# Gathered rows in other homes, weights that wait for a later gather, and a moved wait on the matrix engine

## What is computed

```python
def peer_ffn(x, wq, keys, u, v):
    qry = (xt @ wq).astype(f32).reshape(t, PEER_HEADS, 2, PEER_DK // 2)
    sub = jnp.einsum('thpd,pnd->thpn', qry, keys.astype(f32))
    s_top, i_top = lax.top_k(sub, PEER_TOPK)
    ...
    score, pos = lax.top_k(cand_s, PEER_TOPK)
    idx = jnp.take_along_axis(cand_i, pos, axis=-1)
    gate = jax.nn.softmax(score, axis=-1)
    ...
        act = jax.nn.gelu(jnp.einsum('td,thkd->thk', xb, u[ib]).astype(f32), approximate=False) * gb
        return jnp.einsum('thk,thkd->td', act, v[ib].astype(f32))
    ...
# the third block's input norm and projection, whose weights follow the last gather
h = rms_norm_2(x, g_mix[l])
qa, ka, va, qd, kd, vd, qm = jnp.split(h @ w_in[l], IN_SPLITS, axis=-1)
```

## Time and profile before

| | before |
|---|---|
| median of 3 runs (lowest, highest) | 2308.37 us (2306.19, 2309.63) |
| the profiled execution | 2306.09 us |
| its span, first to last instruction | 2304.3 us |
| busy: PE, DVE, ACT, POOL | 78%, 56%, 37%, 29% of the span |
| moved by the DMA engines | 920.49 MB, mean 399 GB/s |
| of it the gathers' queue (q0) | 549.70 MB |
| TensorE clock granted, mean | 0.853 |

### The profile page before, as it was taken

One profiled execution on the slowest core, in us unless ns is written; L12 is line 12 of the kernel. 1 busy time (PEld: TensorE's weight loads), 2 busy tenths in 40 slices (PEclk: granted clock), 3 DMA queues, 4 the chain that ended last, 5 costly groups with the idle time before them and its releaser, 6 DMA issues.

```text
span 2304.3 us, 30881 instructions
## 1 busy us (share of the span) xinstructions
PE 1789.9 (78%) x11196; PEld 848.4 (37%) x11196; DVE 1298.3 (56%) x3217; ACT 850.6 (37%) x2292; POOL 659.1 (29%) x606
## 2 busy tenths in 40 slices
PE   9999877695797777588779666877779997766666
PEld 4655521161352343153336112343327553222222
DVE  4878887668757766866776867555442331111111
ACT  1324354444445544454744435444333520000000
POOL 1002444434433433533443444333322300000000
PEclk9999887696798888689989667888979999788888
DMA  9988799999999999999999999999999399999998
GB/s 395 381 351 347 314 420 421 420 420 419 388 421 421 421 421 421 421 382 421 412 410 421 421 420 421 421 421 420 421 404 333 121 392 422 428 428 429 428 428 372
DMA packets 111150, 920.49 MB, mean 399 GB/s; under 512 B 12806, under 2 KB 15140, under 8 KB 19044
## 3 DMA queue, kind: packets, MB, share of 16 engines
q0 software_dynamic: 76800, 549.70, 57.9%
q1 hardware_dynamic: 34212, 369.02, 38.8%
HBM read 917.57 MB, written 6.06 MB: 401 GB/s over the span
## 4 chain that ended last, share of the span: by engine, by line
DMA 48%; PE 32%; DVE 10%; ACT 6%; issue 3%; POOL 1%; SPq 0%; DVEq 0%; POOLq 0%; ACTq 0%
DMA arena<-in_peer_uv_dram,arena 27%; DMA arena<-in_moe_pieces_dram 14%; PE summed L1560 8%; DVE y_g L3153 4%; PE gp L1652 3%; PE gp L1105 3%; DMA mod<-in_w_parts_dram 3%; DMA arena<-in_w_slots_dram 2%; PE gp L1967 2%; PE gp L1110 2%; PE gp L1648 2%; DMA arena<-in_w_parts_dram 1%; PE gp L1781 1%; ACT arena L2311 1%; PE gp L1532 1%
## 5 line engine op out<-in xcount | busy, mean ns | idle before, releaser
L1560 PE MATMUL summed<-arena 64*64 64x512 f32 x4096 | 693.8, 773 | 338.5 <-ACT arena L2311 313.9
L3153 DVE CUSTOM_DVE_ANT_0 y_g<-arena,h 128x1024 f32<-128x1024 f32 x512 | 627.3, 1225 | 389.6 <-DMA arena<-in_peer_uv_dram,arena 332.1
L1036 POOL DMA_INDIRECT arena<-in_peer_uv_dram,arena x512 | 592.8, 1158 | 885.9 <-PE summed L1560 805.4
L1560 PEld LDWEIGHTS summed<-arena 64*64 64x64 f32 x4096 | 136.3, 157 | 760.3 <-ACT arena L2311 660.3
L2305 ACT ACTIVATE arena<-arena 128x1 f32<-128x1 f32 x512 | 102.7, 201 | 558.0 <-DVE arena L3153 556.9
L1967 PE MATMUL gp<-arena,mod 128*32 128x512 f32 x1008 | 156.5, 758 | 98.5 <-DMA arena<-in_moe_pieces_dram 98.5
L2311 ACT ACTIVATE arena<-cst,arena 128x128 f32<-128x128 f32 x512 | 205.5, 401 | 16.8
L3546 DVE TENSOR_TENSOR mod<-mod,gp 128x512 f32<-128x512 f32 x8 | 5.5, 687 | 353.7 <-ACT mod L2620 353.7
L2308 ACT ACTIVATE arena<-arena 128x1 f32<-128x1 f32 x512 | 150.8, 294 | 16.6
L1967 PEld LDWEIGHTS gp<-arena,mod 128*32 128x32 f32 x1008 | 31.7, 124 | 214.8 <-DMA arena<-in_moe_pieces_dram 156.8
L2620 ACT ACTIVATE mod<-gp 128x512 f32<-128x512 f32 x8 | 4.8, 597 | 246.7 <-PE gp L1967 246.7
(11 more groups left out here) (530 smaller groups left out, 2339.3 us busy)
## 6 DMA issues: line engine op xcount, KB each, us to landing
arena<-in_moe_pieces_dram SPq DMA_DIRECT2D x92, 2048.0 KB, 25.5
arena<-in_w_slots_dram SPq DMA_DIRECT2D x43, 2048.0 KB, 12.5
arena<-in_w_parts_dram SPq DMA_DIRECT2D x42, 1024.0 KB, 9.3
mod<-in_w_parts_dram SPq DMA_DIRECT2D x23, 1024.0 KB, 9.6
arena<-in_peer_uv_dram,arena POOLq DMA_INDIRECT x512, 15.7
t_rep<-t_rows POOLq DMA_DIRECT2D x1, 3066.0 KB, 18.3
arena<-t_rep POOLq DMA_DIRECT2D x1, 2304.0 KB, 12.8
ext<-in_w_parts_dram SPq DMA_DIRECT2D x2, 1024.0 KB, 22.8
```

Of the source, the lines that this page charges most:

```text
L1036: pool.indirect_dma_start(rowbuf[b], None, a["peer_uv"].rearrange("l n d -> (l n) d"), bass.IndirectOffsetOnAxis(ap=idx[:, col(n):col(n) + ...
L1560: mm = pe.matmul(op[o:o + HALF, b, :], diag[i:i + HALF, n % DIAGS, i:i + HALF], rowbuf[n % ROWS][i:i + HALF, D + b * 512:D + (b + 1) * 512 ...
L3153: v.tensor_tensor_reduce(y[:, t, :], rowbuf[n % ROWS][:, 0:D], h[:, t, :], 1.0, 0.0, ALU.mult, ALU.add, dots[:, c:c + 1]).then_inc(udot, 1)
```

## The change

Five edits. (1) `ROW_HOMES`: gathers with n modulo 8 of 0 and 1 go to slot 1, those of 2 and 3 to slot 0. (2) The turns of the `in2` weights exchange slots 0 and 1 likewise, so `value_slot` is slot 1; each load waits for the same number of summed rows as before. (3) `near` is gather 510 instead of 509: SP's wait of row_in5 becomes one of row_in6. (4) The three waits on `d_hT` move from the round in which PE turns the tile to the round of the first matmul that reads it. (5) ACT takes a root of a constant behind the last row's weighing, into a column that nothing reads.

```diff
-ROW_HOMES = (0, 1, 2, 3, 5, 6, 7, 4)
+ROW_HOMES = (2, 3, 0, 1, 5, 6, 7, 4)
...
-        turns_of = dict(ada=(2, 0, 3, 1), vec=(2, 3), lead=(0, 1), last=(0, 1, 3, 2, 1, 3, 2, 1, 3, 2))
+        turns_of = dict(ada=(2, 0, 3, 1), vec=(2, 3), lead=(0, 1), last=(1, 0, 3, 2, 0, 3, 2, 0, 3, 2))
...
-            near = PICKS - 3
+            near = PICKS - 2
...
                     if s == 5:
                         pe.wait_ge(d_h, 2 * t + 1)
                         turn_tile(h, t)
+                    if s == 9:
                         pe.wait_ge(d_hT, 6 * t + 2)
...
                     if s == 64:
                         pe.wait_ge(d_y, t + 1)
                         turn_tile(y, t)
+                    if s == 67:
                         pe.wait_ge(d_hT, 6 * t + 4)
...
                     if s == 81:
                         pe.wait_ge(d_h, 2 * t + 2)
                         turn_tile(h, t)
+                    if s == 84:
                         pe.wait_ge(d_hT, 6 * t + 6)
...
             rows_to(PICKS)
+            act.activation(small[:, 16:17], eps[:, 0:1], ACT.Sqrt)
             half_square(1, 0, x_ready, 4 * T)
```

## The result

| | median, us | runs |
|---|---|---|
| before | 2309.63 | 15 (2306.19 to 2312.9) |
| changed | 2313.66 | 15 (2311.16 to 2329.76) |

The ratio is 1.0029 with a 95% interval of 1.0018 to 1.0040: slower, by 4 to 9 us, where 2300.3 us was forecast. The profiled execution took 2313.93 us (span 2312.1); the one of before is the fastest of its runs, so the traces lie 7.8 us apart.

A forecast was written before the change was run, and what follows sets the result against it. It took DMA transfers to bound gathers and expert weights, and PE the stretch between. Terms -3.5 - 4.9 + 0.3 = -8.1 us gave 2298.0 against the profiled execution, 2300.3 us as median; range 2295.8 to 2306.0 us.

The forecast's parts named there:

- The moved wait: Inside the gathers, PE's sums start earlier and fill idle DMA time: 2.1 + 2.1 + 0.7 = 4.9 us gained.
- The later weights: End of the gathers: weights issued 2.45 us later, last row summed 2.5 us earlier; `value_slot` lands slightly late, +0.3 us.
- Turned homes: Start of the gathers: gather 0 issued 4.6 us earlier, 0.9 us given back at the ring's end; 3.5 us gained.
- row 8 unchanged at 263: Start of the gathers: row 8's issue stays at 263.03 us, leaving 0.9 us of new idle.
- The second load ... stays hidden: Expert weights: the second load, at 1716.5 before and needed at 1723.7, stays hidden with 2.45 us more.
- The root: ACT, after the last row: a table load of 1.28 us moves into waiting time; nothing gained.
- (C): Expert weights: four loads share engines evenly, `value_slot` lands last; +12.8 instead of +0.3, 2312.8 us; 4%.
- (A): Gathers: consumers, not transfers, set the pace; start worth 1 us, holes half; -3.2 us, 2305.2 us; 20%.
- (B): Expert weights land early enough: -2.5 instead of +0.3, so -10.9 us, 2297.5 us; 12%.
- (D): Start of the gathers: something unseen holds the first gather to 243.7, homes gain nothing; -4.6 us, 2303.8 us; 8%.
- 0.06 for slower: Whole kernel: chance of a slower result, from (C) and what was overlooked; faster by over 0.2% had 0.72.
- The low end of the range: Whole kernel: upper bounds of both gains, less the ring's idle, and half of (B): about -12.5, 2295.8 us.

The follow-up runs named there:

- e1: Changed kernel, but the expert weights wait for the third-last gather again (`near` = 509); ratio 0.9992 to the kernel before.
- e2: Kernel before with only the expert weights' wait moved to the second-last gather (`near` = 510); ratio 1.0050 to the kernel before.
- e4: Changed kernel with `ROW_HOMES` and the turns of the weights as before; ratio 1.0030 to the kernel before.
- f3: Changed kernel with the load of the masks' 2.3 MB table held until both halves of h are normed; ratio 1.0031 to the kernel before.
- g2: f1 with the expert weights released by the fourth-last gather; ratio 1.0007 to the kernel before.
- h1: Kernel before with turned homes, and gathers from 2 on held until slot 0's last vector block is weighed; ratio 0.9987 to the kernel before.
- e6: Kernel before with only the turned homes and the exchanged turns of the weights; ratio 0.9985 to the kernel before.
- f1: e1 with gathers 2 to 7 held until slot 0's last vector block is weighed; ratio 0.9984 to the kernel before.

## Why the prediction was wrong

Two steps failed. The moved wait was to give 4.9 us and gave nothing, since a hole in the mean DMA share was no lost transfer time here. The later weights were to cost 0.3 us and cost 8.5, since the term stops at line 1105 and takes all that comes behind it as hidden.

**Turned homes: -3.5 us.** Alone 3.5 us were won (1.6 to 5.5), so the size came out. Its working did not, which makes that luck so far as the traces tell: it had row 8 unchanged at 263 because "the query projections and their scores stand ahead of it", and did not ask what those wait for. The load of head 4's weights shares the transfer engines with the gathers moved ahead of it. In the changed kernel's profile that took the whole lead.

**The moved wait: -4.9 us.** Measured 0.0001, so +0.2 us (-1.8 to +2.3). The step that failed is "It is less than the idle time, so it counts in full". The mean share of 16 engines fell to 0.43, and I took the missing part for lost transfer time. But a row is whole when its last engine is done. In the hole of the kernel before, from 617 to 618 us, one queue is at work, and the digits of the DMA line (40 slices of this one microsecond) show single packets:

```profile
DMA  0070000000000007000000000007000000000000
...
q0 software_dynamic: 4, 0.02, 5.9%
```

5.9% is one engine of 16 (6.25%). The same at the end of the changed kernel's gathers, from 1703 to 1704 us:

```profile
DMA  0070000000000070000000000070000000000070
...
q0 software_dynamic: 4, 0.03, 7.8%
```

A packet of 8 KB ends every 0.3 us, one behind the other, for 4 us after the other engines have nothing left. Eight of them are the 2.47 us between the dots of rows 509, 510 and 511 (1702.60, 1705.08, 1707.55). Each row ends with 16 writes of 4 bytes in the trace's packets. Fifteen of row 511's have started by 1702.13 us, the sixteenth starts at 1707.06, and 0.5 us later the row is dotted; the last ones of rows 509 and 510, at 1702.13 and 1704.59, stand as far ahead of their dots. So at both places one engine is behind the other fifteen (by 4.9 us at row 511), it works through the hole, and it alone sets when rows land. That it is the same engine at both is not shown, since the trace does not name engines. Why it is behind is open: its packets of 8 KB take 0.31 us, the median of all engines from 1600 to 1700 us. The Trainium skill has both halves of this on the page "DMA: Bandwidth & Descriptors". By its section "Why a DMA increments its semaphore by 16 and not by 1", all 16 engines post a completion of their own for a transfer that GpSimd issues. The trace agrees, with 16 such writes for each row. By its section "Latency and other measured facts", two of the 16 engines are usually slower than the others in traces. The trace shows one that ends last, but not that it is slower. An engine that is behind would also explain why a weight load doubles the distance of row 511 from row 510, 4.92 us instead of 2.47: it has both queues to serve. That is argued, not shown.

**The later weights: +0.3 us.** This term turned the sign: +8.5 us by the ratios of e1 and the changed kernel, +11.5 alone (e2). What it reckoned came about: row 511 was dotted 2.47 us behind row 510, `value_slot` let line 1105 start at 1712.81, line 1110 started 1.3 us earlier as counted from row 510, within my bounds. It failed at "The second load ... stays hidden", where I stopped asking what is late next. The table of the masks comes behind the four loads and lands 3.5 us later, the mask rows behind it 5.8 us later, and DVE's wait of 2.33 us for them was in the trace; only 1.7 us more were covered. With PE's wait of 4.56 us came the half clock, 1.7 us that no term of the prediction had. The sentence that would have caught it stood in the prediction: the stretch from line 1110 to the end should stay 580.6 us, and it became 588.9.

**The root: 0.** Held: 1.0007, with an interval that takes in 1. The table load moved, h was ready earlier, and PE turned it behind the projection as before.

**The rivals.** (C) had the right term and sign and the wrong mechanism: `value_slot` did not land last of four. (A), consumers set the pace, halves the moved wait to -2.5 us, outside the measured interval too, and DVE waited 1.24 us for each of the last rows in the changed kernel, so it was not the consumers that set the pace there. (B) and (D) did not occur. The forecast's 0.06 for slower was too little for a term whose cover I had not followed to its end. The low end of the range is also added up wrong: 5.0 + 5.7 - 0.9 and half of B make some 11 us, not 12.5. The measured time lies above the high end either way.

## What to carry to other kernels

In this kernel a hole in the mean DMA share was not lost time. It can be that only if the transfers behind it are what is waited for, and only if it is in the engine that finishes last; a row is landed by the engine that ends last, so look at what completes, not at the mean. When a batch of loads is released later, follow it to its last member, over all queues, small and late ones included: everything in the batch lands later by the delay, and who has less slack than that is on the path next. A wait of PE can cost more than its length when the granted clock falls behind it; read the clock of the stretch that follows. When transfers are brought forward, look for the small urgent load that now queues behind them.

## What was not expected of the hardware

- At the two places looked at, 617 and 1703 us, one DMA engine was behind the other fifteen, by 4.9 us at the last row, with packets of 8 KB at 0.3 us each; the last rows landed 2.47 us apart, eight of its packets.
- The distance from the table's landing to the use of the masks, 16 loads of 96 KB in pieces of 256 bytes beside six weight loads, was 34.5 to 36.4 us in nine kernels and 37.7 to 43.4 in the changed kernel, e2, e4, f3, g2 and h1. Why it jumps is open; h1 has the early release, so that alone does not do it. In the changed kernel it makes 2.3 of the 6.3 us by which the masks are later. That it also makes the kernels with the late release scatter (2303.8 to 2330.2 us in f3) is a guess; it was not tried by itself.
- The granted clock decided what a wait of PE cost. At the masks it fell to 0.50 in the four kernels in which PE had been idle for 3.28 us or more at a stretch, and in neither with 1.12 or less. At head 4's product it fell within the product behind idle times of 1.82, 1.99 and 2.19 us (e1, changed, e6), the last of several short ones there, and not within it behind 1.81 (f1).
